# Squares of the input kept in four tiles and added behind the last low part, in the openings of a single-core Trainium2 kernel

## The chip, the cores and the metric

The kernel runs on one core of one Trainium2 chip. The metric is the device time of one launch in microseconds (us). The kernel before took 2893.0 us, the median of 3 runs (2892.35 to 2894.73).

## The reference

Six layers of two model blocks, one after the other, on one sequence of 512 tokens with 1024 channels, all in float32. What matters here is how each layer of the second block begins and ends:

```
for i in range(DEPTH_2):                 # 4 layers
    hn = _rms(x, g[0])
    m = conv / pool / differential attention of hn
    x = x + _rms(m, g[1])
    f = _swiglu(_rms(x, g[2]), ffn_w_gate[i], ffn_w_up[i], ffn_w_down[i])
    x = x + _rms(f, g[3])

def _rms(x, g):
    xf = x.astype(jnp.float32)
    y = xf * lax.rsqrt(jnp.mean(xf * xf, axis=-1, keepdims=True) + EPS)
    return (y * g.astype(jnp.float32)).astype(x.dtype)
```

The first block has two layers (dilated window attention, then latent attention), each ended by a layer norm.

## The kernel before, in words

Activations lie transposed in SBUF: 1024 channels are 8 tiles (`KD`) of 128 partitions, with the 512 tokens along the free axis. A float32 product is made of three matmuls on rounded parts: `product` (lines 422 to 424) multiplies the high part of the weight with the high and the low part of the input, and the low part of the weight with the high part of the input. Each is a 128x512 matmul.

**The weight stream.** Weights come as 452 chunks of 512 KB in the order in which they are used, through a ring of 4 places (`RING`). SP starts the transfers. For each chunk ACT copies the rounded high part (`split_hi`, line 415, 128x1024), POOL subtracts it in two halves (line 608) and raises `lo_ready`; PE may then use the chunk. `split_hi` of chunk c waits until PE is done with chunk c-4. On ACT these copies stand in one program order with all its other work: `begin(stage)` makes the high part of the fourth chunk of a stage, and each later `chunk(stage, j)` that of the stage's chunk j+3 (counted from 0).

**Openings.** A stage that starts from x waits for the normalised input tile by tile. At the end of the stage before (`finish`, or `layernorm` in the first block), DVE makes tile t of the new x (line 2139, or 1924), ACT makes its high part `u_hi` (line 1440), DVE makes its low part `u_lo` (`scaled_tile`, line 1950). PE runs `opening` (line 659): for each k it multiplies the k-th tile into four banks, one for each of the stage's first four chunks, so that it follows the tiles as they come. The first six k go bank by bank inside each k; the last two (`late = 2`) go bank after bank: bank 0 with k = 6 and 7, then bank 1, and so on, 6 matmuls for each. There are eight openings: b_lat, conv_in0, up0, up1, c_in, up2, conv_in1 and up3. The last seven have `squares` true.

**The row factor.** `_rms` needs the sum of x squared over all channels. The factor is applied to the products afterwards, so the openings can start without it. In the seven openings ACT squares tile t right behind `u_hi` of that tile (`x_square_to_add`, line 1428): tile 0 into `acc`, the others in turn into the two halves of `sq`. DVE adds them into `acc` (`add_x_square`, line 1959), signals `acc_ready` by a small copy (line 1963), and PE sums over the partitions with a matmul by ones (`pe_sums`, line 464). Before the change that matmul stands behind bank 0 of the opening. ACT then takes the root (`dev_of_added`, line 503) and DVE the reciprocal (line 507), `rs_x`. In ACT's program the root stands ahead of the high part of the fifth chunk. These are ACT's lines for an up stage; in a conv stage and in c_in the root stands ahead of `chunk(stage, 1)` as well:

```
for f in range(2):
    chunk(f"up{layer}", 2 * f, 4 * it)      # f = 0: made by begin
    if first and f == 0:
        dev_of_added(rs_x, eps_rms)
        chunk(f"up{layer}", 1, 0)
```

**Joints.** Between two stages the factor of the stage's output y (or of the layer norm) has to be summed (line 469), rooted by ACT, inverted by DVE (line 2127 or 1914) and spread by PE (line 497, or 655). Around the spread PE runs fillers on idle banks (`keep_busy`, line 480, 256 columns of a product of ones and the identity): 3 ahead of it and 6 behind. There are ten joints: `pe_spread` runs 8 times, `layernorm_sums` twice.

Of the kernel before, what the change touches and what calls it, by code (L numbers as in the profile page):

```python
# [9 lines left out]
ACT = mybir.ActivationFunctionType  # L10
# [4 lines left out]
P = 128  # L15
S = 512
D = 1024
KD = D // P
# [156 lines left out]
def build(nc, stream, ada_w, xT, cols, table, onehot, rope, inv_count, windows, ada_late, out):  # L175
    place = {"at": 16512}

    def sb(name, shape, dt=F32, at=None):
        size = 4 * int(np.prod(shape[1:]))
        if at is None:  # L180
            at = place["at"]
            place["at"] += -(-size // 32) * 32
        assert at + size <= 229344, (name, at + size)
        return nc.alloc_sbuf_tensor_at(name, shape, dt, offset=at)
# [10 lines left out]
    x = sb("x", [P, KD, S])  # L195
# [11 lines left out]
    acc = sb("acc", [P, S], at=sqx_at)  # L207
    sq = sb("sq", [P, 2, S])
# [3 lines left out]
    tmp = sb("tmp", [P, 4, S])  # L212
# [85 lines left out]
    def sem(name):  # L298
        return nc.alloc_semaphore(name)
# [31 lines left out]
    u_ready = sem("u_ready")  # L331
# [4 lines left out]
    sq_ready = sem("sq_ready")  # L336
    sq_used = sem("sq_used")
# [64 lines left out]
    def bank(b, n=S, p0=0, p1=P, at=0):  # L402
        return ps[p0:p1, b, at:at + n]
# [13 lines left out]
    def chunk_tiles(slot, t):  # L417
        return w_hi[:, slot, t * P:(t + 1) * P], w_lo[:, slot, t * P:(t + 1) * P]

    def product(o, w, v, start, stop):  # L420

        nc.tensor.matmul(o, w[0], v[0], start=start, stop=False)  # L422
        nc.tensor.matmul(o, w[0], v[1], start=False, stop=False)  # L423
        return nc.tensor.matmul(o, w[1], v[0], start=False, stop=stop)  # L424

    def u_parts(k):
        return u_hi[:, k, :], u_lo[:, k, :]
# [22 lines left out]
    def group_high_first(pe, o, c, parts):  # L450
# [7 lines left out]
            mm = nc.tensor.matmul(o, chunk_tiles(c % RING, k)[1], parts(k)[0], start=False, stop=k == KD - 1)  # L458
        mm.then_inc(chunk_used, 1)

    def pe_sums(pe, n, src, b=7):

        pe.wait_ge(acc_ready, n)
        pe.matmul(bank(b), ones[:, :], src, start=True, stop=True).then_inc(sums_done, 1)
# [12 lines left out]
    def keep_busy(pe, b, count, width):  # L477

        for _ in range(count):
            pe.matmul(bank(b, width), ones[:, :], bass.AP(ident, 0, [[P, P], [0, width // P], [1, P]]),  # L480
                      start=True, stop=True)

    def pe_factor(pe, n):

        pe.wait_ge(acc_ready, n.up("acc"))
        block_sums(pe, 7, acc, True, False)
        pe.wait_ge(y_last_sq, n.up("last"))
        block_sums(pe, 7, sq[:, 1, :], False, True).then_inc(y_sums, 1)
        pe_spread(pe, n)

    def pe_spread(pe, n):

        keep_busy(pe, 5, 3, 2 * P)
        pe.wait_ge(y_factor, n.up("fin"))
        for b in range(QB):
            r = bass.AP(col, 12 + b, [[32, P], [0, P]])
            mm = pe.matmul(bank(6, P, at=b * P), r, ident[:, :], start=True, stop=True)  # L497
        mm.then_inc(y_spread, 1)
        keep_busy(pe, 5, 6, 2 * P)
# [17 lines left out]
    with nc.Block() as block:  # L517
# [97 lines left out]
        def _(pe):  # L615
            n = Tally()
# [21 lines left out]
            def sum_x_columns(t, b):  # L638

                pe.wait_ge(sqx_ready, n.up("sqx"))  # L640
                block_sums(pe, b, sqx[:, t % 2, :], t == 0, t == KD - 1).then_inc(sqx_summed, 1)

            def layernorm_sums(layer):

                pe.wait_ge(acc_ready, n.up("acc"))
                pe.matmul(bank(7), ones[:, :], acc[:, :], start=True, stop=False)
                pe.wait_ge(out_evac, KD * (layer + 1))
                pe.matmul(bank(7), ones[:, :], x[:, KD - 1, :], start=False, stop=True).then_inc(sums_done, 1)
                for t in range(KD):
                    sum_x_columns(t, 6)  # L650
                keep_busy(pe, 4, 3, 2 * P)
                pe.wait_ge(ln_factor, layer + 1)
                for b in range(QB):
                    r = bass.AP(col, 12 + b, [[32, P], [0, P]])
                    mm = pe.matmul(bank(5, P, at=b * P), r, ident[:, :], start=True, stop=True)
                mm.then_inc(ln_spread, 1)
                keep_busy(pe, 4, 6, 2 * P)

            def opening(c0, squares):

                n.up("u", KD)
                late = 2
                for k in range(KD - late):
                    pe.wait_ge(u_ready, n["u"] - KD + k + 1)
                    for j in range(4):
                        if k == 0:
                            pe.wait_ge(lo_ready, c0 + j + 1)
                        product(bank(j), chunk_tiles((c0 + j) % RING, k), u_parts(k), k == 0, False)
                pe.wait_ge(u_ready, n["u"])
                for j in range(4):  # L670
                    for k in range(KD - late, KD):
                        mm = product(bank(j), chunk_tiles((c0 + j) % RING, k), u_parts(k), False, k == KD - 1)
                    mm.then_inc(chunk_used, 1)
                    if j == 0 and squares:
                        pe_sums(pe, n.up("acc"), acc[:, :])

            n.up("u", KD)
            for t in range(KD + 1):
# [10 lines left out]
                if t:  # L689
                    k = t - 1  # L690
# [162 lines left out]
            for m in range(2, KD):  # L853
                if m >= 4:
                    pe.wait_ge(out_evac, m - 3)
                for k in range(KA):
                    mm = a_out_tile(m, k)
                    if (KA * m + k) % TPC == TPC - 1 and k < KA - 1:
                        mm.then_inc(chunk_used, 1)
                mm.then_inc(chunk_used if m == KD - 1 else grp_done, 1)  # L860
            layernorm_sums(0)


            opening(BASE["b_lat"], False)
            group(pe, bank(4), BASE["b_lat"] + 4, 0, [(0, k, u_parts(k)) for k in range(KD)])
            for g in range(NPAIR):
                if g >= 2:
                    pe.wait_ge(gate_ready, G0 + g - 1)
                group(pe, bank(5 + g % 2), BASE["b_gate"] + g, 0, [(0, k, u_parts(k)) for k in range(KD)])
                if g == 1:  # L870
                    pe_sums(pe, n.up("acc"), acc[:, :])
                    pe_sums(pe, n.up("acc"), sq[:, 0, :], 0)
# [102 lines left out]

            out8(BASE["b_out"], KD, lambda k: pe.wait_ge(m_split, KA + k + 1))
            layernorm_sums(1)


# [106 lines left out]
            pool_sum(KD - 2)  # L1086
            pool_sum(KD - 1)
            pe_spread(pe, n)
            ffn(1)

# [163 lines left out]
        def _(act):  # L1254
            n = Tally()
# [167 lines left out]

            def x_square_to_add(t):

                if t >= 3:
                    act.wait_ge(sq_used, n.get("squ", 0) + t - 1)
                nc.scalar.activation(sq[:, t % 2, :] if t else acc[:, :], x[:, t, :], ACT.Square).then_inc(sq_ready, 1)
                if t == KD - 1:
                    n.up("squ", KD)  # L1430

# [264 lines left out]
        def _(dve):  # L1696
            n = Tally()
# [41 lines left out]
            for t in range(KD + 1):  # L1739
# [4 lines left out]
                if t:  # L1744
                    k = t - 1
# [160 lines left out]
            def layernorm(layer, nxt_scaled):  # L1906
# [26 lines left out]
                if nxt_scaled is None:  # L1933
                    modulated_lo(KD - 1)
                    n.up("u", KD)
                    dve.wait_ge(u_ready, n["u"])
                next_parts(nxt_scaled, KD)

            def add_square(dst, t, last):
# [6 lines left out]
            def scaled_tile(layer, which, t):  # L1946

                dve.wait_ge(u_hi_ready, n.up("u_hi"))
                g0 = norm_col(layer, which, t)
                nc.vector.scalar_tensor_tensor(out=u_lo[:, t, :], in0=x[:, t, :], scalar=par[:, g0:g0 + 1],  # L1950
                                               in1=u_hi[:, t, :].bitcast(F32), op0=ALU.mult,
                                               op1=ALU.subtract).then_inc(u_ready, 1)

            def add_x_square(t):

                if t > 1:
                    dve.wait_ge(sq_used, n["sq"])
                dve.wait_ge(sq_ready, n.up("sq", 2 if t == 1 else 1))
                nc.vector.tensor_tensor(acc[:, :], acc[:, :], sq[:, t % 2, :],
                                        ALU.add).then_inc(sq_used, 2 if t == 1 else 1)  # L1960
                if t == KD - 1:
                    dve.wait_ge(sq_used, n["sq"])
                    nc.vector.tensor_copy(col[:, 31:32], acc[:, 0:1]).then_inc(acc_ready, 1)

            def next_parts(nxt, t):

                if nxt is None:
                    return
                layer, which, added = nxt
                if t == KD and added:  # L1970
                    add_x_square(KD - 2)
                if t >= 1:
                    scaled_tile(layer, which, t - 1)
                if added and t == KD:
                    add_x_square(KD - 1)
                elif added and t >= 3:
                    add_x_square(t - 2)

            dve.wait_ge(m_split, KA)
            ch(nc.vector.memset(acc[:, :], 0.0))  # L1980
# [589 lines left out]
```

## Time and profile before

| | |
|---|---|
| median of 3 runs | 2893.0 us (2892.35 to 2894.73) |
| the profiled execution | 2891.97 us |
| its span, first to last instruction | 2890.1 us |
| PE busy with matmuls | 2820.2 us, 98% of the span |
| DVE, POOL, ACT busy | 1399.8, 1244.1 and 927.6 us |
| mean granted TensorE clock | 0.998 |
| DMA | 100 GB/s over the span |

A wait is read from the bracket behind a row in order of time: the idle time of the engine just ahead of that instruction, and the instruction that released it. Matmuls overlap, so the pace of PE is the distance of their starts and not their durations.

### The profile page before, as it was taken

How to read it: one execution, taken by the hardware profiler on the slowest of the kernel's cores; microseconds unless marked ns; L12 is line 12 of the kernel's file. 1: busy time of each engine (PE TensorE's matmuls, PEld its weight loads, DVE VectorE, ACT ScalarE, POOL GpSimd, SP SyncE). 2: the span in 40 equal slices, each digit the busy share in tenths (PEclk: the TensorE clock that was granted, in tenths of full speed). 3: DMA queues.
4: the chain of work that ended last, by engine and by line, in shares of the span. 5: the costliest groups of instructions: out<-in, count | busy, mean ns of one | idle time of the engine just before them, and what ended most of it. 6: DMA issues, size and time to landing. Idle time of an engine off the chain costs nothing.

```text
span 2890.1 us, 37064 instructions
## 1 busy us (share of the span) xinstructions
PE 2820.2 (98%) x13786; PEld 2365.0 (82%) x13786; DVE 1399.8 (48%) x2001; ACT 927.6 (32%) x1291; POOL 1244.1 (43%) x913
## 2 busy tenths in 40 slices
PE   7999999999999999999999999999999999999998
PEld 5888877888787888888888878987888878788886
DVE  4444556775755444036443066546442074554412
ACT  3333424663213222243222233333222231332222
POOL 1453335113443545433545433334454545354544
PEclk9999999999999999999999999999999999999999
DMA  7654224102322333332333322222333323233333
GB/s 266 177 189 135 79 72 136 34 23 66 86 89 73 110 97 99 102 115 73 95 94 102 107 82 80 65 66 81 101 94 102 104 86 95 73 104 100 94 102 95
DMA packets 106123, 284.98 MB, mean 99 GB/s; under 512 B 38669, under 2 KB 38797, under 8 KB 104675
## 3 DMA queue, kind: packets, MB, share of 16 engines
q1 hardware_dynamic: 99360, 257.64, 30.0%
q10 hardware_dynamic: 6643, 25.64, 2.6%
q8 instruction: 88, 1.44, 0.2%
q14 instruction: 32, 0.26, 0.0%
HBM read 280.98 MB, written 8.85 MB: 100 GB/s over the span
## 4 chain that ended last, share of the span: by engine, by line
issue 54%; POOL 32%; PE 12%; POOLq 1%; DVE 0%; DMA 0%; ACT 0%; ACTq 0%
POOL w_lo L608 32%; PE ps L422 4%; PE ps L423 4%; PE ps L424 4%; DMA hot<-in_onehot 0%; POOLq L606 0%; POOLq L166 0%; PE ps L623 0%; DVE x L2139 0%; DVE tmp L2133 0%; PE ps L469 0%; PE ps L480 0%; ACT w_hi L415 0%; PE ps L497 0%; ACTq L1257 0%
## 5 line engine op out<-in xcount | busy, mean ns | idle before, releaser
L608 POOL TENSOR_TENSOR w_lo<-w_raw,w_hi 128x512 fp32r<-128x512 f32 x904 | 1243.2, 1398 | 1632.6 <-ACT w_hi L415 1632.6
L422 PE MATMUL ps<-u_hi,w_hi 128*128 128x512 f32 x2232 | 878.6, 394 | 26.0 <-DVE u_lo L1950 18.7
L424 PE MATMUL ps<-u_hi,w_lo 128*128 128x512 f32 x2232 | 870.2, 390 | 0.0
L423 PE MATMUL ps<-u_lo,w_hi 128*128 128x512 f32 x2232 | 870.1, 390 | 0.0
L415 ACT ACTIVATE w_hi<-w_raw 128x1024 fp32r<-128x1024 f32 x452 | 475.3, 1055 | 817.8 <-PE ps L424 777.0
L422 PEld LDWEIGHTS ps<-u_hi,w_hi 128*128 128x128 f32 x2232 | 419.9, 188 | 123.4 <-DVE u_lo L1950 24.5
L424 PEld LDWEIGHTS ps<-u_hi,w_lo 128*128 128x128 f32 x2232 | 419.8, 188 | 88.5
L423 PEld LDWEIGHTS ps<-u_lo,w_hi 128*128 128x128 f32 x2232 | 420.1, 188 | 87.2 <-issue 1.9
L424 PE MATMUL ps<-h_hi,w_lo 128*128 128x512 f32 x704 | 273.9, 389 | 0.0
L422 PE MATMUL ps<-h_hi,w_hi 128*128 128x512 f32 x704 | 273.9, 389 | 0.0
L423 PE MATMUL ps<-h_lo,w_hi 128*128 128x512 f32 x704 | 273.9, 389 | 0.0
L2166 DVE TENSOR_TENSOR tmp<-ps,rs_x 128x512 f32<-128x512 f32 x88 | 60.7, 690 | 369.3 <-PE ps L424 369.3
L2150 DVE COPY y<-ps 128x512 f32<-128x512 f32 x49 | 33.9, 692 | 388.5 <-PE ps L424 388.2
L1575 ACT ACTIVATE tmp<-tmp 128x512 f32<-128x512 f32 x88 | 55.7, 632 | 413.2 <-DVE tmp L2164 413.2
L424 PEld LDWEIGHTS ps<-h_hi,w_lo 128*128 128x128 f32 x704 | 132.2, 188 | 27.7
L423 PEld LDWEIGHTS ps<-h_lo,w_hi 128*128 128x128 f32 x704 | 132.2, 188 | 27.6
L422 PEld LDWEIGHTS ps<-h_hi,w_hi 128*128 128x128 f32 x704 | 132.2, 188 | 27.0
L1767 DVE TENSOR_TENSOR h_lo<-tmp,h_hi 128x512 f32 (+1 forms) x88 | 140.7, 1599 | 8.7
L1766 DVE CAST h_hi<-tmp 128x512 f32 (+1 forms) x88 | 107.4, 1220 | 10.6 <-DVE tmp L2168 8.6
L422 PE MATMUL ps<-m_hi,w_hi 128*128 128x512 f32 x248 | 97.1, 392 | 0.9 <-DVE m_lo L2323 0.6
L424 PE MATMUL ps<-m_hi,w_lo 128*128 128x512 f32 x248 | 96.6, 389 | 0.0
L1549 ACT ACTIVATE sq<-y 128x512 f32<-128x512 f32 x57 | 36.1, 633 | 188.3 <-DVE y L2150 180.1
(293 smaller groups left out, 3373.0 us busy)
## 6 DMA issues: line engine op xcount, KB each, us to landing
w_raw<-in_stream SPq DMA_DIRECT2D x452, 512.0 KB, 3.6
late_ring<-in_ada_late ACTq DMA_DIRECT2D x32, 512.0 KB, 4.9
ada_ring<-in_ada SPq DMA_DIRECT2D x8, 1024.0 KB, 7.9
dilated_bias_rows<-dilated_bias SPq DMA_DIRECT2D x18, 244.1 KB, 4.7
band_a<-dilated_bias_rows SPq DMA_DIRECT2D x96, 28.0 KB, 2.0
x<-in_x SPq DMA_DIRECT2D x8, 256.0 KB, 5.8
bias_rows<-bias_scratch ACTq DMA_DIRECT2D x4, 512.0 KB, 7.9
out_yT<-x SPq DMA_DIRECT2D x8, 256.0 KB, 2.0
```

The source lines that it names most:

```text
L415: nc.scalar.activation(w_hi[:, slot, :], w_raw[:, slot, :], ACT.Copy).then_inc(hi_ready, 1)
L422: nc.tensor.matmul(o, w[0], v[0], start=start, stop=False)
L423: nc.tensor.matmul(o, w[0], v[1], start=False, stop=False)
L424: return nc.tensor.matmul(o, w[1], v[0], start=False, stop=stop)
L608: ins = nc.gpsimd.tensor_tensor(w_lo[:, s, half], w_raw[:, s, half], w_hi[:, s, half].bitcast(F32), ALU.subtract)
L1549: nc.scalar.activation(sq[:, m % 2, :], y[:, m, :], ACT.Square).then_inc(sq_ready, 1)
L1575: nc.scalar.activation(tmp[:, f, :], tmp[:, f, :], ACT.Silu).then_inc(g_silu, 1)
L1766: ch(nc.vector.tensor_copy(hi, src))
L1767: nc.vector.tensor_tensor(lo, src, hi.bitcast(F32), ALU.subtract).then_inc(signal, 1)
L2150: nc.vector.tensor_copy(y[:, m, :], bank(b)).then_inc(out_evac, 1)
L2166: ch(nc.vector.tensor_tensor(tmp[:, 2 + f, :], bank(at + 1), rs_x[:, :], ALU.mult))
```

## The change

Four things change, all around the joints and openings.

- ACT writes the squares of tiles 1 to 7 in turn into four places, the two halves of `sq` and the first two of `tmp`: tiles 1, 4 and 5 into `sq`, tiles 2, 3, 6 and 7 into `tmp`. It waits for a place from tile 5 on instead of from tile 3 on.
- DVE adds tile 1 behind low part 3 and tile 2 behind low part 5. The other five are added behind low part 7, the last.
- In `opening` the wait for the last low part goes from in front of bank 0's last two k to in front of its k = 7, and `pe_sums` stands behind bank 2 (the third) instead of bank 0.
- `keep_busy` ahead of the spread runs 2 fillers instead of 3, in `pe_spread` and in `layernorm_sums`.

```
+    def x_square_tile(t):
+        return sq[:, t % 2, :] if t % 4 < 2 else tmp[:, t % 2, :]
...
     def pe_spread(pe, n):
-        keep_busy(pe, 5, 3, 2 * P)
+        keep_busy(pe, 5, 2, 2 * P)
...
                 for t in range(KD):
                     sum_x_columns(t, 6)
-                keep_busy(pe, 4, 3, 2 * P)
+                keep_busy(pe, 4, 2, 2 * P)
...
-                pe.wait_ge(u_ready, n["u"])
                 for j in range(4):
                     for k in range(KD - late, KD):
+                        if j == 0:
+                            pe.wait_ge(u_ready, n["u"] - KD + k + 1)
                         mm = product(bank(j), chunk_tiles((c0 + j) % RING, k), u_parts(k), False, k == KD - 1)
                     mm.then_inc(chunk_used, 1)
-                    if j == 0 and squares:
+                    if j == 2 and squares:
                         pe_sums(pe, n.up("acc"), acc[:, :])
...
             def x_square_to_add(t):
-                if t >= 3:
-                    act.wait_ge(sq_used, n.get("squ", 0) + t - 1)
-                nc.scalar.activation(sq[:, t % 2, :] if t else acc[:, :], x[:, t, :], ACT.Square).then_inc(sq_ready, 1)
+                if t >= 5:
+                    act.wait_ge(sq_used, n.get("squ", 0) + t - 3)
+                nc.scalar.activation(x_square_tile(t) if t else acc[:, :], x[:, t, :], ACT.Square).then_inc(sq_ready, 1)
...
-                nc.vector.tensor_tensor(acc[:, :], acc[:, :], sq[:, t % 2, :],
+                nc.vector.tensor_tensor(acc[:, :], acc[:, :], x_square_tile(t),
...
-                if t == KD and added:
-                    add_x_square(KD - 2)
                 if t >= 1:
                     scaled_tile(layer, which, t - 1)
-                if added and t == KD:
-                    add_x_square(KD - 1)
-                elif added and t >= 3:
-                    add_x_square(t - 2)
+                if added and t == 4:
+                    add_x_square(1)
+                elif added and t == 6:
+                    add_x_square(2)
+                elif added and t == KD:
+                    for k in range(3, KD):
+                        add_x_square(k)
```

**DVE at the end of the opening of up0, before.** x += is line 2139, the low part line 1950, the addition of a square line 1959:

```order
L1950 SCALAR_TENSOR_TENSOR u_lo<-x,par,u_hi 128x512 [waits u_hi_ready]
L1959 TENSOR_TENSOR acc<-acc,sq 128x512 [waits sq_ready,sq_used]
L2139 TENSOR_TENSOR x<-x,tmp 128x512 [waits vec_step]
L1959 TENSOR_TENSOR acc<-acc,sq 128x512 [waits sq_ready,sq_used]
L1950 SCALAR_TENSOR_TENSOR u_lo<-x,par,u_hi 128x512 [waits u_hi_ready]
L1959 TENSOR_TENSOR acc<-acc,sq 128x512 [waits sq_ready,sq_used]
L1963 COPY col<-acc 128x1 [waits sq_used]
```

The same place in the changed kernel, where these are lines 2144, 1954 and 1963:

```order
L1954 SCALAR_TENSOR_TENSOR u_lo<-x,par,u_hi 128x512 [waits u_hi_ready]
L2144 TENSOR_TENSOR x<-x,tmp 128x512 [waits vec_step]
L1954 SCALAR_TENSOR_TENSOR u_lo<-x,par,u_hi 128x512 [waits u_hi_ready]
L1963 TENSOR_TENSOR acc<-acc,tmp 128x512 [waits sq_ready,sq_used]
L1963 TENSOR_TENSOR acc<-acc,sq 128x512 [waits sq_ready,sq_used] x2
L1963 TENSOR_TENSOR acc<-acc,tmp 128x512 [waits sq_ready,sq_used] x2
L1967 COPY col<-acc 128x1 [waits sq_used]
```

Two additions stood ahead of the last low part and one behind it; now none stands between the last two low parts and five stand behind the last one.

**PE at the end of the same opening, before**, from the first product of bank 0's last two k to the start of bank 1's:

```order
L422 MATMUL ps<-u_hi,w_hi 128x512 [waits u_ready]
L423 MATMUL ps<-u_lo,w_hi 128x512
L424 MATMUL ps<-u_hi,w_lo 128x512
L422 MATMUL ps<-u_hi,w_hi 128x512
L423 MATMUL ps<-u_lo,w_hi 128x512
L424 MATMUL ps<-u_hi,w_lo 128x512
L464 MATMUL ps<-acc,ones 128x512 [waits acc_ready]
L422 MATMUL ps<-u_hi,w_hi 128x512
```

In the changed kernel, from the last product of bank 2 to the first of the fifth chunk:

```order
L422 MATMUL ps<-u_hi,w_hi 128x512
L423 MATMUL ps<-u_lo,w_hi 128x512
L424 MATMUL ps<-u_hi,w_lo 128x512
L467 MATMUL ps<-acc,ones 128x512 [waits acc_ready]
L422 MATMUL ps<-u_hi,w_hi 128x512
L423 MATMUL ps<-u_lo,w_hi 128x512
L424 MATMUL ps<-u_hi,w_lo 128x512
L422 MATMUL ps<-u_hi,w_hi 128x512
L423 MATMUL ps<-u_lo,w_hi 128x512
L424 MATMUL ps<-u_hi,w_lo 128x512
L422 MATMUL ps<-u_hi,w_hi 128x512 [waits chunk_lo_ready]
```

Before, 18 matmuls stood between the sum and the fifth chunk; now 6 do. The matmul of the sum has moved 12 places down in a list that is otherwise the same.

## Rows read from the trace of the kernel before

**Rows 1.** The page, part 1: busy us (share of the span) xinstructions.
```profile
PE 2820.2 (98%) x13786; PEld 2365.0 (82%) x13786; DVE 1399.8 (48%) x2001; ACT 927.6 (32%) x1291; POOL 1244.1 (43%) x913
```

**Rows 2.** Waits of PE, whole run: us in total, times, longest.
```profile
PE ps L422 <- DVE u_lo L1950: 18.7, 14, 1.7
...
PE ps L422 <- POOL w_lo L608: 2.4, 8, 0.7
```

**Rows 3.** PE in order of time, opening of up1: start, duration, [idle <-releaser].
```profile
1333.84 0.39 PE L424 MATMUL ps<-u_hi,w_lo 128*128 128x512 f32 x1
1335.63 0.50 PE L422 MATMUL ps<-u_hi,w_hi 128*128 128x512 f32 x1 [1.40 <-DVE u_lo L1950]
...
1337.12 1.02 PE L464 MATMUL ps<-acc,ones 128*128 128x512 f32 x2
...
1338.21 0.40 PE L423 MATMUL ps<-u_lo,w_hi 128*128 128x512 f32 x1
...
1341.85 0.39 PE L424 MATMUL ps<-u_hi,w_lo 128*128 128x512 f32 x1
1342.49 0.50 PE L422 MATMUL ps<-u_hi,w_hi 128*128 128x512 f32 x1 [0.25 <-POOL w_lo L608]
```

**Rows 4.** ACT in order of time, the same opening.
```profile
1338.18 0.69 ACT L503 ACTIVATE rs_x<-ps,eps_rms 128x512 f32<-128x512 f32 x1 [2.87 <-PE ps L464]
1338.77 1.05 ACT L415 ACTIVATE w_hi<-w_raw 128x1024 fp32r<-128x1024 f32 x1
```

**Rows 5.** POOL in order of time, the same opening.
```profile
1339.89 2.54 POOL L608 TENSOR_TENSOR w_lo<-w_raw,w_hi 128x512 fp32r<-128x512 f32 x2 [24.45 <-ACT w_hi L415]
```

**Rows 6.** DVE in order of time, the same opening, its end.
```profile
1332.75 0.68 DVE L1959 TENSOR_TENSOR acc<-acc,sq 128x512 f32<-128x512 f32 x1
1333.35 0.68 DVE L2139 TENSOR_TENSOR x<-x,tmp 128x512 f32<-128x512 f32 x1
1333.95 0.69 DVE L1959 TENSOR_TENSOR acc<-acc,sq 128x512 f32<-128x512 f32 x1
1334.82 0.75 DVE L1950 SCALAR_TENSOR_TENSOR u_lo<-x,par,u_hi 128x512 fp32r<-128x512 f32 x1 [0.19 <-ACT u_hi L1440]
1335.49 0.68 DVE L1959 TENSOR_TENSOR acc<-acc,sq 128x512 f32<-128x512 f32 x1
1336.21 0.15 DVE L1963 COPY col<-acc 128x1 f32<-128x1 f32 x1
```

**Rows 7.** PE, opening of conv_in0, after the layer norm.
```profile
735.16 0.39 PE L424 MATMUL ps<-u_hi,w_lo 128*128 128x512 f32 x1
737.30 0.50 PE L422 MATMUL ps<-u_hi,w_hi 128*128 128x512 f32 x1 [1.75 <-DVE u_lo L1950]
...
738.79 1.02 PE L464 MATMUL ps<-acc,ones 128*128 128x512 f32 x2
...
744.16 0.50 PE L422 MATMUL ps<-u_hi,w_hi 128*128 128x512 f32 x1 [0.26 <-POOL w_lo L608]
```

**Rows 8.** PE, opening of c_in, up to the turned factors.
```profile
1707.47 1.02 PE L464 MATMUL ps<-acc,ones 128*128 128x512 f32 x2
...
1712.78 0.66 PE L630 MATMUL ps<-ident,rs_x 128*128 128x128 f32 x4 [0.17 <-DVE col L2246]
```

**Rows 9.** PE at the joint ahead of up0.
```profile
898.46 1.46 PE L480 MATMUL ps<-ident,ones 128*128 128x256 f32 x6
899.76 1.05 PE L497 MATMUL ps<-ident,col 128*128 128x128 f32 x8
```

**Rows 10.** DVE at the same joint.
```profile
899.03 0.18 DVE L2127 RECIPROCAL col<-col 128x4 f32<-128x4 f32 x1 [0.82 <-ACT col L1557]
```

**Rows 11.** PE behind its longest pause at the full clock.
```profile
110.07 0.50 PE L422 MATMUL ps<-ka_hi,qa_hi 64*128 64x512 f32 x1 [3.05 <-ACT va L1369]
```

**Rows 12.** Busy time by stretch there; PEclk is the granted clock's share.
```profile
110.00:116.00 6.00, 5.93 (x22) 4.84 (x23) 2.58 (x8) 4.10 (x9) 4.77 (x4) 0.72 0.78 289
```

**Rows 13.** PE, opening of b_lat, its first wait.
```profile
416.06 0.50 PE L422 MATMUL ps<-u_hi,w_hi 128*128 128x512 f32 x1 [1.93 <-DVE u_lo L1736]
```

## The prediction

> **What bounds the kernel now.** I read the page's busy shares first: PE has matmuls in flight for 98% of the span, with DVE, ACT and POOL under half [rows 1]. A change can only pay where PE waits, and costs wherever PE waits more. So the next view is the list of PE's waits [rows 2]. It shows 18.7 us in 14 waits for a low part of the input, and 2.4 us in 8 waits for POOL's low part of a chunk. The 14 are two in each of the seven openings that add squares: one ahead of the first product, one ahead of k = 6.
>
> The third view is PE in order of time through one opening, up1 [rows 3]. PE ends k = 5 with a matmul started at 1333.84 and starts k = 6 at 1335.63, after 1.40 us idle. The sum over the partitions starts at 1337.12. Then 18 matmuls follow at 0.2275 us (from the second of bank 1 at 1338.21 to the last of bank 3 at 1341.85 are 16 steps). The fifth chunk starts at 1342.49, and it too has waited: 0.25 us, for POOL. The reader should stop at this last bracket, because it says that PE's arrival at the fifth chunk is not what decides its start.
>
> What decides it is read upwards through three engines. POOL's two halves run from 1339.89 to 1342.43, after 24 us of idleness, released by ACT [rows 5]. ACT's high part of that chunk starts at 1338.77, directly behind the root of the sum at 1338.18, and the root was released by PE's sum after 2.87 us of ACT idle [rows 4]. In ACT's program the root stands ahead of that high part, so the copy cannot start before the sum is done, although its place in the ring is free as soon as bank 0 is finished. From the start of the sum to the start of the fifth chunk is therefore a fixed chain: 1342.49 - 1337.12 = 5.37 us. In conv_in0 it is 744.16 - 738.79 = 5.37 us again [rows 7]. In c_in the chain goes through the reciprocal to the turning of the factors: 1712.78 - 1707.47 = 5.31 us, with a wait of 0.17 us [rows 8]. At all seven places the start of the sum sets when PE goes on.
>
> **The change part by part.**
>
> *The additions behind the last low part.* DVE's starts are 0.60 us apart where an addition stands between other work (1332.75 to 1333.35) [rows 6]. Six additions stand ahead of the last low part before, two after. One of the four that leave stood in the latency between x += and the low part, where the low part still waited 0.19 us for ACT; the others give 3 x 0.60 = 1.8 us. The last low part of up1 then starts at 1334.82 - 1.8 = 1333.02 and ends at 1333.8. PE ends k = 5 at about 1334.07 (1333.84 + 0.23) and asks for the last low part 3 matmuls later still. So PE's wait ahead of k = 6 goes altogether: 1.79 us between starts becomes 0.23, and the first matmul after a wait, which takes 0.34 to its successor instead of 0.23, loses that too. That is 1.67 us. In conv_in0 it is 737.30 - 735.16 - 0.23 + 0.11 = 2.02 us [rows 7].
>
> *The sum behind the third bank.* It moves down by two banks, 12 matmuls: 12 x 0.2275 = 2.73 us later in PE's own work. Against the earlier k = 6 the sum starts 2.73 - 1.67 = 1.06 us later in the clock of the kernel; with the actual starts (k = 6 at 1334.07, 18 matmuls of 0.2275 behind it) it is 1338.17 against 1337.12, 1.05 us. For conv_in0 it is 735.39 + 4.10 = 739.49 against 738.79, 0.7 us. The waits ahead of k = 6 in the other five lie within 0.04 us of up1's, so I take 1.0 for six openings. Everything that follows hangs on the sum: the root, the high part, POOL, PE. So the fifth chunk starts later by the same amount: 6 x 1.0 + 0.7 = **6.7 us lost**. PE gets to the fifth chunk 1.67 us earlier, and stands there: the pause grows from 0.25 to 0.25 + 2.73 = 2.98 us (bank 3 alone, not three banks, now covers the chain).
>
> *Are the five additions in time?* Chained, they start 0.72 us apart (1335.49 to 1336.21) [rows 6]. The first starts 0.67 behind the last low part, at 1333.69; the copy starts at 1333.69 + 3.60 = 1337.29 and ends at 1337.44, 0.7 us before PE asks at 1338.17. In conv_in0 the same sum leaves 0.4 us. The square of tile 7 waits on ACT until tile 3 has been added, done at 1334.4, and needs 0.6; its own addition comes at 1336.57. The extra places cost nothing, and PE's wait for `acc_ready` stays covered by bank 2. If that cover went, each tenth would be added at all seven.
>
> *One filler less.* At the joint ahead of up0 three fillers take 899.76 - 898.46 = 1.30 us, 0.43 each [rows 9]. With two, PE is free at 899.33. DVE's reciprocal ends at 899.03 + 0.18 = 899.21 [rows 10], and a matmul starts 0.06 us behind its release (1335.57 to 1335.63 [rows 3, 6]), so the filler is nearly all on the path. The spread gains between 0.2 us (if the factor's weights can no longer be loaded ahead) and 0.43; I take 0.3, nearer to the whole filler less the 0.11 of a first matmul after a wait. All of DVE's work at a joint follows the spread, so the gain is kept: 10 x 0.3 = **3.0 us won** (2.0 to 4.3).
>
> *The clock.* The new pauses are a kind that the kernel nearly lacks. Its longest pause at the full clock is 3.05 us, ahead of the matmul at 110.07 [rows 11]. After it the clock falls to half: from 110 to 116 us the granted share is 0.72, so 0.28 x 6 = 1.7 us is lost [rows 12]. The next longest, 1.93 us, ahead of b_lat's first product [rows 13], leaves it at full. A pause of 2.98 us lies close to the one that cost the clock. Nothing in the trace says how often it falls at such a length. The ends are none of seven and seven of seven, 0 and 11.9 us; because one case nearly as long did fall I take half, 3.5 x 1.7 = **6.0 us lost**.
>
> The sum is 6.7 - 3.0 + 6.0 = +9.7 us. The profiled execution took 2891.97 us (span 2890.1), so it would take 2901.7; the median of the runs stands 1.0 us above it, at 2893.0, and goes to **2902.7 us**.
>
> **The rivals.**
>
> *The clock holds at the new pauses.* The chain binds as above, but no pause is long enough: +3.7 us, 2896.7 us. For it speaks that 1.93 us did no harm and that no pause forecast here reaches 3.05. Against it, one pause 0.07 us longer did harm. A single fall would give 2898.4. A rule bears on this: the Trainium skill, page "TensorE: Matmul & The Clock Gate", section "HAM oscillation — how this bites in real kernels", blames only pauses longer than any forecast here. By that rule the time is this rival's; the trace does not agree, as the clock fell behind 3.05 us, which the section's bound would also have let pass.
>
> *PE's arrival sets the fifth chunk (the other side).* If ACT could make the fifth chunk's high part once bank 0 is done, the wait that goes would be won whole: 7 x 1.7 + 3.0 = 14.9 us, 2878.1 us. It decides where POOL ends before PE has finished bank 3. Against it speaks that POOL's wait is there in the profile before, that ACT sat idle 2.87 us ahead of the root while bank 0's place was free or about to be, and that the change leaves ACT's list as it is.
>
> *The sum itself is late.* If the squares or the additions ran 1.5 us behind my times, the sum would start 0.8 us later still in each opening: 5.6 us more, 2908.3 us. The slack of 0.7 and 0.4 us speaks against it.
>
> **How the numbers follow.** A measurement of this kernel can tell about 0.2%, 5.8 us, from no change, so the border is at 2898.8. My forecast, the chain with two falls of the clock or more, has 0.68, the late sum 0.05: slower 0.73. The clock that holds, or falls once, has 0.22: within 0.2%. PE's arrival has 0.05: faster. The range runs from no fall and whole fillers (+6.7 - 4.3 = +2.4, 2895.4) to seven falls and the least of the fillers (+6.7 - 2.0 + 11.9 = +16.6, 2909.6): 2895.4 to 2909.6. It leaves out the faster rival, and nothing else of weight.
>
> **What would show it.** PE's waits for low parts fall from 14 to about 7 and lose some 10 us, each opening without a pause ahead of k = 6. POOL's waits at the fifth chunk grow to about 3 us each, six of them, with one for the turned factors in c_in. The sum starts 1.0 us later, and sum to fifth chunk stays 5.37. The granted clock shows half-rate stretches of some 3 us directly behind some of these pauses. The distance from fillers to spread shrinks from 1.30 to about 1.0. It is wrong if the fifth chunk starts earlier than before relative to the opening's first product, or if the joints lose what the fillers gave.

## The result, and the profile after

| | before | changed |
|---|---|---|
| median | 2892.35 us (5 runs, 2888.96 to 2894.73) | 2906.38 us (5 runs, 2903.44 to 2912.08) |
| profiled execution | 2891.97 us | 2903.44 us |
| span of the profile | 2890.1 us | 2901.6 us |
| mean granted clock | 0.998 | 0.994 |

The ratio of the runs is 1.0054, with a 95% interval of 1.0043 to 1.0065. The changed kernel is slower by 0.54%, clear of the 0.2% that a measurement can tell from nothing. Forecast was 2902.7 us, with a range of 2895.4 to 2909.6. The profiled execution is the fastest of the five; the others have a mean granted clock of 0.992 to 0.994.

PE's waits in the changed kernel, the view that answers to [rows 2] (line numbers above 458 are up to 5 higher than before):

```profile
PE ps L422 <- POOL w_lo L611: 17.8, 7, 2.9
...
PE ps L422 <- DVE u_lo L1954: 11.1, 7, 1.6
...
PE ps L633 <- DVE col L2251: 2.9, 1, 2.9
```

The 14 waits for low parts are 7 now: the seven ahead of k = 6 are gone. The total falls by 7.6 us and not by the forecast 10, since each of the seven ahead of a first product has grown, in up1 from 1.18 to 1.62 us. POOL's waits, 2.4 us in 8 before, are 17.8 us in 7, each up to 2.9 us, and the turned factors of c_in cost a wait of 2.9 us where they cost 0.17. What the change removed from one place stands in full size at the next, and is larger there.

The opening of up1 on PE, as in [rows 3]: first product, last product of bank 2, the sum, bank 3, fifth chunk.

```profile
1318.98 0.50 PE L422 MATMUL ps<-u_hi,w_hi 128*128 128x512 f32 x1 [1.62 <-DVE u_lo L1954]
...
1339.30 0.39 PE L424 MATMUL ps<-u_hi,w_lo 128*128 128x512 f32 x1
1339.53 1.02 PE L467 MATMUL ps<-acc,ones 128*128 128x512 f32 x2
...
1341.53 0.39 PE L424 MATMUL ps<-u_hi,w_lo 128*128 128x512 f32 x1
1344.83 0.50 PE L422 MATMUL ps<-u_hi,w_hi 128*128 128x512 f32 x1 [2.91 <-POOL w_lo L611]
```

From 1318.98 PE runs without a gap to the sum at 1339.53, and stands still for 2.91 us after bank 3. First product to fifth chunk is 1344.83 - 1318.98 = 25.85 us. Before, the first product was this row:

```profile
1317.59 0.50 PE L422 MATMUL ps<-u_hi,w_hi 128*128 128x512 f32 x1 [1.18 <-DVE u_lo L1950]
```

With the fifth chunk at 1342.49 [rows 3] that made 24.90 us. The chain behind the sum, as in [rows 4] and [rows 5]:

```profile
1340.58 0.69 ACT L506 ACTIVATE rs_x<-ps,eps_rms 128x512 f32<-128x512 f32 x1 [4.17 <-PE ps L467]
1341.17 1.05 ACT L415 ACTIVATE w_hi<-w_raw 128x1024 fp32r<-128x1024 f32 x1
```

```profile
1342.29 2.48 POOL L611 TENSOR_TENSOR w_lo<-w_raw,w_hi 128x512 fp32r<-128x512 f32 x2 [25.45 <-ACT w_hi L415]
```

ACT takes the root 1.05 us behind the start of the sum, the high part of the fifth chunk directly behind it, POOL its two halves, and PE starts 5.30 us behind the sum (before: 5.37). ACT had been idle for 4.17 us ahead of the root, and for some 3.6 us of these bank 0's place in the ring was free (its last matmul started at 1336.58). DVE's end of the opening, as in [rows 6]:

```profile
1334.39 0.75 DVE L1954 SCALAR_TENSOR_TENSOR u_lo<-x,par,u_hi 128x512 fp32r<-128x512 f32 x1 [0.79 <-ACT u_hi L1444]
1335.07 0.68 DVE L1963 TENSOR_TENSOR acc<-acc,tmp 128x512 f32<-128x512 f32 x1
1335.78 1.42 DVE L1963 TENSOR_TENSOR acc<-acc,sq 128x512 f32<-128x512 f32 x2
1337.23 1.42 DVE L1963 TENSOR_TENSOR acc<-acc,tmp 128x512 f32<-128x512 f32 x2
1338.69 0.15 DVE L1967 COPY col<-acc 128x1 f32<-128x1 f32 x1
```

The last low part starts at 1334.39, five additions follow 0.72 us apart, and the copy ends at 1338.84, 0.7 us before PE's sum. That part came out to the tenth.

Where the time went, by stage. A stage is measured from one spread of factors to the next on PE (line 497 or 655, now 500 or 658):

| stage | before | changed | difference | clock at half behind its pause |
|---|---|---|---|---|
| conv 0 | 185.74 | 186.36 | +0.62 | no |
| up and down 0 | 370.26 | 372.74 | +2.48 | yes |
| pool | 42.75 | 42.68 | -0.07 | (no such opening) |
| up and down 1 | 370.28 | 372.88 | +2.60 | yes |
| attention (c) | 265.63 | 267.52 | +1.89 | yes |
| up and down 2 | 370.31 | 371.34 | +1.03 | no |
| conv 1 | 185.38 | 187.68 | +2.30 | yes |
| up and down 3 | 370.30 | 372.57 | +2.27 | yes |

The eight come to +13.1 us. The stretch ahead of the first of them ran 2.1 us shorter in this execution, which is why its span grew by 11.5 us only. The stages with an opening split in two kinds, and the clock is what splits them. Stretches of 6 us behind the pauses (columns: stretch, its length, busy time of each engine, granted clock, DMA share, GB/s):

```profile
743.00:749.00 6.00, 5.89 (x26) 4.88 (x27) 5.83 (x6) 0.37 (x2) 6.00 (x6) 1.00 0.61 175
928.00:934.00 6.00, 4.62 (x14) 3.70 (x15) 5.73 (x7) 1.64 (x3) 3.71 (x4) 0.72 0.29 87
1344.00:1350.00 6.00, 5.17 (x16) 4.12 (x17) 5.72 (x8) 1.97 (x3) 3.70 (x3) 0.72 0.30 87
1716.50:1722.50 6.00, 4.54 (x25) 4.14 (x26) 5.79 (x8) 2.75 (x3) 6.00 (x5) 0.72 0.46 128
1984.00:1990.00 6.00, 4.73 (x21) 3.91 (x22) 5.73 (x8) 1.58 (x2) 3.70 (x3) 1.00 0.27 87
2355.00:2361.00 6.00, 4.38 (x13) 3.54 (x14) 5.83 (x6) 1.83 (x2) 6.00 (x6) 0.72 0.43 114
2542.50:2548.50 6.00, 4.29 (x13) 3.48 (x14) 5.72 (x7) 1.98 (x3) 3.70 (x4) 0.72 0.30 87
```

0.72 over 6 us is a stretch of 3.4 us at half rate, 1.2 instead of 2.4 GHz. It stands behind five of the seven pauses. The openings of conv_in0 and up2 had the same pause, 2.93 and 2.92 us, and kept the clock. Two more such stretches, at 69 and 110 us, lie in the first attention layer; before there was the one near 111 us.

### The profile page after: what moved, and what is told of

Same layout as the page of the kernel before. It is cut to its first block, busy times and chain, and to the rows that moved or that the text cites. A ratio compares the mean times of both kernels' runs of the same rounds, so it can differ in the third digit from the quotient of the medians.

```text
span 2901.6 us, 37024 instructions
## 1 busy us (share of the span) xinstructions
PE 2822.3 (97%) x13766; PEld 2366.7 (82%) x13766; DVE 1407.4 (49%) x2001; ACT 928.1 (32%) x1291; POOL 1242.2 (43%) x913
## 4 chain that ended last, share of the span: by engine, by line
issue 55%; POOL 32%; PE 12%; POOLq 1%; DVE 0%; DMA 0%; ACT 0%; ACTq 0%
POOL w_lo L611 32%; PE ps L422 4%; PE ps L423 4%; PE ps L424 4%; DMA hot<-in_onehot 0%; POOLq L609 0%; POOLq L166 0%; PE ps L626 0%; DVE x L2144 0%; DVE tmp L2138 0%; PE ps L472 0%; ACT w_hi L415 0%; PE ps L500 0%; PE ps L483 0%; ACTq L1261 0%
## 5 line engine op out<-in xcount | busy, mean ns | idle before, releaser
L423 PE MATMUL ps<-m_lo,w_hi 128*128 128x512 f32 x248 | 96.5, 389 | 0.0
```

## The experiments

All ratios are against the kernel before, run on the same chip.

### One filler less, alone

```
-        keep_busy(pe, 5, 3, 2 * P)
+        keep_busy(pe, 5, 2, 2 * P)
```

and the same in `layernorm_sums`.

> The kernel before with one filler less ahead of the spread, nothing else. The prediction's filler term says 0.3 us won at each of ten joints, 3.0 us in all (ratio 0.9990). The theory formed on the profile after says nothing is won: the spread starts 0.43 us earlier, but the first x += of the joint ends 0.54 us behind POOL's low part of the fourth chunk whatever its own start is, so its row grows from 1.35 to about 1.75 us and the first product of the opening keeps its distance of 7.1 us from the sum over y (ratio 1.0000, within 0.5 us).

Measured: ratio 1.0003 (0.9994 to 1.0012), medians 2893.47 against 2890.96 us. Nothing is won. Its DVE and POOL at the joint ahead of up0:

```profile
899.25 0.18 DVE L2127 RECIPROCAL col<-col 128x4 f32<-128x4 f32 x1 [0.82 <-ACT col L1557]
900.68 0.75 DVE L2133 SCALAR_TENSOR_TENSOR tmp<-y,par,ps 128x512 f32<-128x512 f32 x1 [1.25 <-PE ps L497]
901.46 1.75 DVE L2139 TENSOR_TENSOR x<-x,tmp 128x512 f32<-128x512 f32 x1
```

```profile
900.17 2.49 POOL L608 TENSOR_TENSOR w_lo<-w_raw,w_hi 128x512 fp32r<-128x512 f32 x2 [3.59 <-ACT w_hi L415]
```

The kernel before at the same place:

```profile
900.85 0.75 DVE L2133 SCALAR_TENSOR_TENSOR tmp<-y,par,ps 128x512 f32<-128x512 f32 x1 [1.65 <-PE ps L497]
901.63 1.35 DVE L2139 TENSOR_TENSOR x<-x,tmp 128x512 f32<-128x512 f32 x1
```

```profile
899.95 2.49 POOL L608 TENSOR_TENSOR w_lo<-w_raw,w_hi 128x512 fp32r<-128x512 f32 x2 [3.59 <-ACT w_hi L415]
```

With three fillers the first x += starts 0.78 us behind the scaled y and lasts 1.35 us, to 902.98; with two it starts 0.39 us earlier against the reciprocal and lasts 1.75 us. In both it ends 0.55 us behind POOL's last element of the fourth chunk (902.44 and 902.66). The reader should see that a DVE row that grows by just what its start came earlier is not slow work but a wait without a bracket. POOL's start hangs on ACT's high part, which hangs on the root, and on no filler. The Trainium skill, page "GPSIMD Engine Reference", section "1. Specifications", lists POOL's interfaces to SBUF as shared with DVE, with contention for DVE instructions that have two inputs there, and the Trainium skill's page "SBUF — State Buffer", section "SBUF: two separate sides", calls that an exclusive lock, by which the later one is stopped for the whole of the other's instruction. The trace agrees, as x += (two inputs in SBUF) is stretched and the scaled y, which reads the factor from PSUM, is not (0.75 us beside POOL).

The same holds at every opening with squares: from the spread to the first product it is 4.82 to 4.89 us in the kernel before and 5.25 to 5.33 in this one and in the changed kernel, so the whole filler of 0.43 us comes off ahead of the spread and is lost again before the first product. Stage by stage the profile with two fillers is within 0.03 us of the one before wherever the clock held. It did not hold everywhere: this profile has five half-rate stretches, before had one. They begin at 69, 298, 414, 738 and 1277 us, and the three stretches between spreads that hold the last three are 1.5, 1.1 and 1.3 us longer. The one at 414 us lies at b_lat's first product, whose pause has grown from 1.93 to 2.33 us with the shorter joint. Over all runs the mean granted clock is 0.9966 (11 runs) against 0.9976 before (17 runs). So the missing filler wins nothing at the full clock, and may cost a little of the clock; no run tells that apart from chance.

### The sum back behind the first bank

```
-                    if j == 2 and squares:
+                    if j == 0 and squares:
```

> The changed kernel with the sum back behind the first bank. Chain theory (sum, root, high part, POOL, fifth chunk): the sum now waits for the additions and starts about 0.3 us later than before the change instead of 1.05, the fifth chunk follows 5.37 us behind it, the pause in front of it is 0.25 to 0.6 us, and the clock falls behind none of the openings: before plus 2 us, some 12 us faster than the changed kernel. Rival, that the five additions behind the last low part and the squares in tmp are what costs: the place of the sum does not matter and it stays at plus 14 us.

Measured: ratio 1.0031 (1.0020 to 1.0043), 2899.63 us, that is 8.9 us over before, not 2. PE in the opening of up1, and the clock behind three of its pauses:

```profile
1337.42 1.13 PE L467 MATMUL ps<-acc,ones 128*128 128x512 f32 x2 [1.91 <-DVE col L1967]
...
1342.90 0.50 PE L422 MATMUL ps<-u_hi,w_hi 128*128 128x512 f32 x1 [0.23 <-POOL w_lo L611]
```

```profile
734.00:740.00 6.00, 3.92 (x9) 2.49 (x10) 3.01 (x5) 1.63 (x2) 0.09 (x1) 0.72 0.00 0
922.00:928.00 6.00, 5.12 (x14) 3.60 (x15) 3.63 (x3) 2.92 (x3) 1.84 (x2) 0.72 0.01 4
1337.00:1343.00 6.00, 5.35 (x21) 3.78 (x21) 3.99 (x4) 2.92 (x3) 2.55 (x2) 1.00 0.01 3
```

The mechanism is as expected: the sum waits for the copy of the additions (1.91 us), the fifth chunk follows 5.48 us behind it with a pause of 0.23 us, and first product to fifth chunk is 25.4 us, 0.5 over before, 3.5 us for seven. The rival falls, since the place of the sum alone takes 6 to 7 us back. What I had missed is the clock: the wait at the sum is a pause of about 2 us, and behind it the clock fell in four of seven openings of the profile (the pauses are 2.33, 1.97, 1.97 and 1.94 us; it held behind 1.91, 1.97 and 1.98). In that profile the three stages that kept the clock are 0.51 to 0.54 us longer than before and the four others 1.20 to 1.58, so a fall costs 0.7 to 1.1 us here; together the seven stages give 7.4 us, 3.6 for the later sum and 3.8 for the falls. The profiled execution, 2896.23 us, is the fastest of the seven runs, and the others have a lower mean clock (0.992 to 0.995 against 0.996); their additional falls would make up the rest, but they were not profiled. So a pause of 2 us can cost the clock, which the prediction had taken for harmless after one of 1.93 us [rows 13].

### The sum behind the third bank, alone

The same line in the kernel before, `j == 0` to `j == 2`, and nothing else.

> The kernel before with the sum behind the third bank and nothing else: squares, additions and the wait ahead of k = 6 as they were. Chain theory: the sum starts 2.73 us later in each of seven openings, 19.1 us, and as the pauses ahead of the fifth chunk are again 2.98 us the clock falls behind most of them (five at 1.4 us, 7 us): plus 26 us. Rival, that the additions cost: within 3 us of before.

Measured: ratio 1.0092 (1.0078 to 1.0105), 2918.05 us, plus 27 us. Its waits, and the sum and fifth chunk of up1:

```profile
PE ps L422 <- DVE u_lo L1950: 18.8, 14, 1.8
PE ps L422 <- POOL w_lo L608: 18.7, 9, 2.9
```

```profile
1348.88 1.02 PE L464 MATMUL ps<-acc,ones 128*128 128x512 f32 x2
...
1354.19 0.50 PE L422 MATMUL ps<-u_hi,w_hi 128*128 128x512 f32 x1 [2.92 <-POOL w_lo L608]
```

PE still waits 18.8 us for low parts, and 18.7 us for POOL on top; sum to fifth chunk is 5.31 us. The additions are where they were, so they are not what costs. The place of the sum does, by 12 matmuls in each opening and by the clock behind the pauses. The stages show the two apart: the two whose openings kept the clock (conv 1, and up and down 3) are 2.74 and 2.70 us longer than before, which is 12 matmuls of 0.2275, and the five with a half-rate stretch are 4.2 to 4.35 us longer.

### The pause filled

```
+                if squares:
+                    keep_busy(pe, 6, 5, 2 * P)
```

behind the last product of `opening`, in the changed kernel.

> The changed kernel with five more fillers on an idle bank behind the opening's last product, 5 x 0.43 = 2.15 us of the 2.92 us in which PE waits for the fifth chunk. No work that counts is moved. Theory that part of the loss is the clock: the fifth chunk starts where it did in the changed kernel, the pause left is some 0.8 us, and the clock falls behind none of the seven: only the later sum is left, 6 to 7 us over before (ratio 1.0022 against 1.0054 for the changed kernel). Rival, that the falls do not hang on these pauses: ratio stays 1.0054.

Measured: ratio 1.0023 (1.0014 to 1.0033), 2897.74 us. The clock behind the seven filled pauses:

```profile
743.00:749.00 6.00, 5.22 (x23) 3.98 (x23) 5.79 (x7) 1.60 (x2) 6.00 (x6) 1.00 0.50 116
930.00:936.00 6.00, 5.31 (x23) 4.38 (x24) 5.73 (x8) 2.10 (x3) 3.71 (x3) 1.00 0.27 87
1345.00:1351.00 6.00, 5.24 (x23) 4.17 (x23) 5.72 (x8) 1.85 (x3) 3.70 (x3) 1.00 0.32 87
1716.50:1722.50 6.00, 4.57 (x36) 4.33 (x37) 5.79 (x8) 2.26 (x3) 6.00 (x5) 1.00 0.55 162
1982.00:1990.00 8.00, 7.24 (x32) 5.71 (x31) 7.54 (x9) 3.46 (x5) 4.80 (x4) 1.00 0.24 66
2354.00:2360.00 6.00, 5.22 (x23) 3.97 (x23) 5.79 (x7) 1.38 (x2) 6.00 (x5) 1.00 0.50 130
2540.00:2547.00 7.00, 6.24 (x28) 4.85 (x27) 6.57 (x8) 2.47 (x5) 4.51 (x4) 1.00 0.28 75
```

All seven keep the full clock, and the fifth chunk starts where it did: 25.8 to 25.9 us behind the first product in the six openings that a fifth chunk follows, as in the changed kernel. The profile can be read by stage as above: 186.41, 371.25, 371.32, 266.54, 371.29, 186.46 and 371.27 us for the seven stages with such an opening, 6.6 us more than before in all, which is the later sum. The five stages of the changed kernel that lost the clock are 1.49, 1.56, 0.98, 1.22 and 1.30 us longer than these, 6.55 us together. The runs agree: the mean granted clock is 0.993 over the changed kernel's five and 0.997 over this one's nine. The difference between this kernel and the changed one, 1.0054 - 1.0023 = 0.0031 or 9 us, is what the clock costs in the runs; the 0.0023 left, 6.6 us, is the later sum. These are the two terms of the prediction, measured apart. The ratios stem from different chips, so the 9 us are good to some 4 us (both intervals).

### The high parts ahead of the root

```
                         if first and f == 0:
+                            for c in range(1, 4):
+                                chunk(f"up{layer}", c, 0)
                             dev_of_added(rs_x, eps_rms)
-                            chunk(f"up{layer}", 1, 0)
```

with the copies skipped further down, `dev_of_added` behind `chunk(stage, 3)` of a conv stage (counted from 0, so behind the same three copies), and `j == 0` for the sum of c_in.

> The changed kernel, but on ACT the high parts of the fifth, sixth and seventh chunk stand ahead of the root of the sum in the up and conv stages; in c_in, where the factor itself is waited for, the sum goes back behind the first bank. Chain theory: in six openings the fifth chunk no longer waits for the sum, so PE runs through: first product to fifth chunk 22.8 us instead of 24.9 (before) and 25.85 (changed), c_in 0.5 us over before. 12 us under before, 2879 us or a ratio of 0.9958; less if the additions, which now run beside POOL, make the sum late. Rival, that the pause has another cause such as POOL's own backlog or the squares: as the changed kernel, plus 14 us.

Measured: ratio 0.9960 (0.9947 to 0.9973), 2879.89 us. This is faster than both kernels, by 11 us than before and by some 27 than the changed one (from the ratios, on different chips). The end of up1's opening on PE, ACT and POOL:

```profile
1336.82 1.02 PE L467 MATMUL ps<-acc,ones 128*128 128x512 f32 x2
...
1338.82 0.39 PE L424 MATMUL ps<-u_hi,w_lo 128*128 128x512 f32 x1
1339.05 0.39 PE L422 MATMUL ps<-u_hi,w_hi 128*128 128x512 f32 x1
```

```profile
1334.36 1.06 ACT L415 ACTIVATE w_hi<-w_raw 128x1024 fp32r<-128x1024 f32 x1 [0.64 <-PE ps L424]
...
1338.04 0.67 ACT L506 ACTIVATE rs_x<-ps,eps_rms 128x512 f32<-128x512 f32 x1
```

```profile
1335.49 7.84 POOL L611 TENSOR_TENSOR w_lo<-w_raw,w_hi 128x512 fp32r<-128x512 f32 x6 [21.37 <-ACT w_hi L415]
```

No pause is left in this opening behind its first product. POOL starts 1.33 us ahead of the sum instead of 2.76 us behind it, and PE goes from the last product of bank 3 into the fifth chunk at 0.23 us: 1339.05 - 1316.27 = 22.8 us from the first product. The only things moved are ACT's copies (and c_in's sum), so the changed kernel's pause was the root standing ahead of the copy. PE's table of waits named POOL; the culprit stood two engines up, in ACT's program order. By stage, the four up and down stages are each 2.24 to 2.30 us shorter than before, conv 0 and conv 1 by 1.75 and 2.19 us. The attention stage, where only the sum went back, is 1.2 us longer and not the 0.5 expected: PE waits 1.97 us at the sum, and the clock fell behind it. The kernel before with its own place of the sum and additions, and only ACT's copies moved, was not run; how much of the gain needs the earlier low parts is not shown.

### POOL out of the joint

In the kernel before, `begin(stage)` moves behind the first tile's square, and PE takes bank 3's k = 0 and 1 last of the first two k.

> The kernel before, but in the seven openings with squares ACT makes the high part of the fourth chunk behind the first tile's square instead of ahead of all tiles, and PE takes bank 3's k = 0 and 1 after the other three banks' k = 0 and 1. POOL theory: the first x += takes 0.7 instead of 1.35 us, the opening's first product starts about 1.0 us nearer to the sum over y than 7.1 us, and since POOL's work moves beside later additions where DVE is ahead of PE, most of it is kept: 5 to 7 us faster than before (ratio 0.998). Rival, that x += is long for another reason, or that POOL then stops DVE at a worse place: no gain, or slower by up to 1 us per opening.

Measured: ratio 1.0038 (1.0025 to 1.0052), 2902.76 us, some 11 us slower. A miss, and its DVE rows say why:

```profile
905.31 0.69 DVE L2144 TENSOR_TENSOR x<-x,tmp 128x512 f32<-128x512 f32 x1
...
910.08 1.77 DVE L2144 TENSOR_TENSOR x<-x,tmp 128x512 f32<-128x512 f32 x1
```

```profile
908.31 2.99 POOL L608 TENSOR_TENSOR w_lo<-w_raw,w_hi 128x512 fp32r<-128x512 f32 x2 [8.28 <-ACT w_hi L415]
```

The first x += is down to 0.69 us, as expected, and the first product comes 0.67 us nearer. But POOL stops DVE a little later: the third x += lasts 1.77 us and ends at 911.85, again 0.55 us behind POOL. With the additions where they were, the low parts had no room to take that, and PE's wait ahead of k = 6 grew from 1.4 to 2.4 us. From spread to sum up1 takes 25.66 us instead of 24.35. The longer pauses cost the clock too: in the profile it fell behind six of the seven (2.4 to 2.5 us each), whose stages are 2.1 to 2.4 us longer than before, while the one that kept it, up and down 2, is 0.9 us longer. This profiled execution is the slowest of its five runs (2909.03 us, mean granted clock 0.992; the others 0.994 and 0.995). The stop moved, it did not go.

### Both

The "last kernel" of this expectation is the one with the copies ahead of the root; the move out of the joint, with PE's new order of the first two k, is added to it.

> The last kernel and, with it, the fourth chunk's high part behind the first tile's square as in the experiment on POOL in the joint. There the first product came 0.7 us nearer but was given back ahead of k = 6; here the low parts have room, so it should be kept, and with two fillers a little more: 0.7 to 1.0 us at seven joints, 5 to 7 us under the last kernel, 2873 us. Rival, that POOL's work merely stops DVE elsewhere: within 2 us of the last kernel.

Measured: ratio 0.9979 (0.9970 to 0.9987), 2885.06 us: 5 us slower than without the move in the joint. DVE at the end of the opening of up0:

```profile
922.65 1.42 DVE L1970 TENSOR_TENSOR acc<-acc,sq 128x512 f32<-128x512 f32 x2
924.10 2.39 DVE L1970 TENSOR_TENSOR acc<-acc,tmp 128x512 f32<-128x512 f32 x2
926.53 0.15 DVE L1974 COPY col<-acc 128x1 f32<-128x1 f32 x1
```

The last two additions take 2.39 us instead of 1.42: POOL starts at 924.31, while the first of them runs and is not stretched (0.69 us), and the second, started beside it, lasts 1.67 us. The opening began 1.07 us earlier against the spread, so POOL's low part of the fifth chunk, now early, reached the additions and stopped them; PE waited 0.97 us at the sum. I had named this for the next kernel and not for this one.

> The last kernel with the sum behind the fourth bank instead of the third (c_in as there). If the additions are late because POOL's low part of the fifth chunk stops them, PE waits up to 1 us at the sum behind the third bank and not behind the fourth: 3 to 6 us under the last kernel. If they are in time: within 1 us of it.

Measured: ratio 0.9958 (0.9945 to 0.9970), 2879.81 us, 5 us under the last one, within what was expected. It is no better than the kernel with the copies ahead of the root alone. Of the 1.07 us won at a joint only 0.2 stays: from the fillers of the joint ahead of up0 to those ahead of the pool stage, a stretch in which neither profile has a half rate, it takes 367.8 us against 368.0. PE starts earlier and then waits 0.3 us for the second low part, among others: up0's first product to fifth chunk takes 23.4 us against 22.8, so 0.65 us of the 1.07 are gone there. I have not followed the rest.

## Why the prediction was right

*The wait ahead of k = 6 goes.* Right: 7 waits for low parts are left of 14. In up1 the sum starts 20.55 us behind the first product instead of 19.53, with 12 matmuls or 2.73 us more ahead of it, so 1.71 us went, where 1.67 was forecast; and the additions are in time by the 0.7 us forecast.

*The sum's place moves a fixed chain.* Right, and the heart of it. Forecast was a loss of 6.7 us. The two openings that kept the clock give 0.62 and 1.03 us where 0.7 and 1.0 were forecast, and the kernel with the pause filled measures 6.6 us. What the prediction got from reading one bracket of 0.25 us (PE's arrival is not what sets the fifth chunk) the kernel with the copies ahead of the root shows on the chip.

*One filler less.* Wrong: "10 x 0.3 = 3.0 us won" failed, and measured 0.0003 of the time over before, between 1.7 us won and 3.5 lost. One of the prediction's own signs of being wrong, "if the joints lose what the fillers gave", came true. The step that failed is "all of DVE's work at a joint follows the spread, so the gain is kept". The spread does start earlier, by a whole filler (at up0's joint it stands 0.87 us behind the first filler instead of 1.30, where 1.0 was forecast); the first x += then waits for POOL. The rows that say so were in the profile before: an addition of 0.68 us that lasts 1.35 there.

*The clock.* That these pauses cost the clock was right, and the size a little small: "half, 3.5 x 1.7 = 6.0 us". The half was a guess from one case, as the prediction said, and that it came this near is partly luck. In the profile five pauses of seven cost the clock. Less 0.95 us for the later sum (the rise of 24.90 to 25.85), the five stages give 1.5, 1.65, 0.95, 1.35 and 1.3 us, 6.8 us together or 1.35 each and not 1.7. The pair of kernels with and without fillers gives 6.55 us in the same way, and 9 us by the ratios of their runs. In the profiles the sum closes: 6.6 us for the later sum, 6.55 for the clock and nothing for the fillers are the 13.1 us of the table. So the prediction had too high a price for a fall and too few falls. The error of the fillers, 3.0, and that of the clock, 1 to 3, add up to the 4 us by which the sum of +9.7 fell short of the measured +14.0. By the rule that was weighed, of the Trainium skill's page "TensorE: Matmul & The Clock Gate", section "HAM oscillation — how this bites in real kernels", none of these pauses would have counted; the trace does not agree.

*The rivals.* That the clock holds is out, by five rows at 0.72. That PE's arrival sets the fifth chunk is out for this kernel, and true once ACT's order is changed. That its 2878.1 us is near the 2879.9 that the kernel with the copies ahead took is luck: it counted 3.0 us of fillers that were not won and a gain in c_in, which lost 1.2 us, while the openings of the up stages gave 2.2 to 2.3 us each and not 1.7; and the kernel before ran at 2890.8 us on that chip. That the sum is late did not happen here, and happened in the kernel with both moves, by POOL stopping the additions.

## What to carry to other kernels

Before a wait is removed, look at the next bracket behind it on the same engine: if that one is not zero, its chain sets the time, and what moves the head of that chain is what counts. Follow it upwards, and look at the program order of each engine on it for work that could start earlier than the instruction ahead of it, since an order can cost as much as a dependency. And where a row lasts longer by what its start gained, something outside its waits decides when it ends. A profile is one execution: where the clock falls by chance, compare it stage by stage, and count the falls in each, before a total is split into terms.

## What the runs showed of the hardware

- An instruction of DVE with two inputs in SBUF that starts while one of POOL's subtractions runs ends some 0.55 us behind the end of that subtraction (x += and the additions of squares): 0.68 us becomes 1.35, 1.67, 1.75 or 1.77. One that was already running when POOL started kept its 0.69 us (at 924.10 us in the kernel with both moves), and POOL's two halves then took 2.99 or 3.31 us instead of 2.49. No wait shows it.
- The clock fell to half rate for 3.4 us behind pauses of 2.9 us in five cases of seven in the changed kernel and again in five of seven with the sum moved alone, and behind pauses of 1.91 to 2.33 us at the sum in four of seven. At b_lat's first product it held twice and fell once behind a pause of 1.92 or 1.93 us, and with two fillers, where that pause is 2.33 us, it fell in five profiles of seven. The shortest pause of an opening behind which it fell is 1.78 us (one filler less, at 738 us). No length of pause separates the cases. One fall costs some 0.7 to 1.6 us here by stage, 1.35 in the mean of the changed kernel, less than the 1.7 us that 3.4 us at half rate would lose, as part of it falls beside work that PE waits for anyway; that last reason is argued, not tested.
- Fillers of PE with no use otherwise, in a pause of 2.9 us that they did not lengthen, took the loss from 0.54% to 0.23%, some 9 us.
